# RWKV recurrence of a two-block model: token rows by chunk parity instead of by head, operands turned by whole 128x128 transposes, Gram products in two banks

## The reference, cut to what matters

```python
def frame_step(state, inp):                      # state: 64x64 for each head
    r_t, w_t, k_t, v_t, a_t, b_t = inp
    sa = einsum('bhvk,bhk->bhv', state, a_t)
    state = state * w_t + sa[..., None] * b_t + v_t[..., None] * k_t
    y_t = einsum('bhvk,bhk->bhv', state, r_t)
    return state, y_t
...
a, b = -kk, kk * ah                              # kk: k * k_k, normed in each head
y = (y - mean) * rsqrt(var + GN_EPS) * ln_w + ln_b
bonus = sum(rh * kh * r_k, axis=-1, keepdims=True) * vh
out = ((y + bonus) * g) @ w_o
```

## Time and profile before

| | us |
|---|---|
| median of 3 timed runs | 2976.05 (2974.72 to 2978.09) |
| span of the profiled execution | 2971.7 |
| TensorE matmul busy in it | 2867.8 (97%) |
| DVE, ACT, POOL busy | 1571.3, 1040.2, 185.7 |
| mean granted TensorE clock | 0.983 of full speed |
| one stage of the recurrence (stages 1 to 6) | 39.62 |
| TensorE busy in one such stage | 37.80 |
| DVE, ACT, POOL busy in it | 28.16, 12.02, 10.17 |

### The profile page before, as it was taken

How to read it: one execution, slowest core, us unless ns; L and a number is a source line. 1 busy time by engine, 2 the same in 40 slices (tenths; PEclk the granted TensorE clock), 3 DMA queues, 4 the chain that set the end, 5 groups by cost and what they waited for, 6 DMA issues and landing times.

```text
span 2971.7 us, 47531 instructions
## 1 busy us (share of the span) xinstructions
PE 2867.8 (97%) x21368; PEld 2323.2 (78%) x21368; DVE 1571.3 (53%) x2210; ACT 1040.2 (35%) x1333; POOL 185.7 (6%) x159
## 2 busy tenths in 40 slices
PE   7999999999899989999999999899999998999999
PEld 6878888778888877888777767678888786788887
DVE  7766554463677654323366666554344546454342
ACT  4225233343233235334343232242222446532221
POOL 0010000201322100000200000010000000100000
PEclk9999999999999999999999999899999999999999
DMA  7545544120000022222220111022322220222322
GB/s 280 217 170 197 199 178 173 66 99 29 17 3 3 18 102 84 99 99 99 82 72 30 51 36 44 15 100 82 110 95 83 100 86 1 85 100 70 122 82 68
DMA packets 41388, 270.70 MB, mean 91 GB/s; under 512 B 4576, under 2 KB 4832, under 8 KB 13280
## 3 DMA queue, kind: packets, MB, share of 16 engines
q1 hardware_dynamic: 40752, 266.11, 25.1%
q10 hardware_dynamic: 432, 1.54, 0.1%
HBM read 265.54 MB, written 2.10 MB: 90 GB/s over the span
## 4 chain that ended last, share of the span: by engine, by line
PE 89%; DVE 7%; ACT 3%; issue 1%; DMA 0%; SPq 0%; DVEq 0%; ACTq 0%
PE ps L696 21%; PE ps L702 21%; PE ps L697 21%; PE ps L2195 6%; PE ps L2973 1%; PE ps L1757 1%; PE ps L1740 1%; PE ps L1751 1%; PE ps L2301 1%; PE ps L2360 1%; PE ps L2354 1%; DVE WL L408 1%; PE ps L2329 1%; PE ps L2890 1%; PE ps L2877 1%
## 5 line engine op out<-in xcount | busy, mean ns | idle before, releaser
L696 PE MATMUL ps<-HH,WH 128*128 128x512 f32 x1928 | 765.9, 397 | 18.7 <-ACT HH L672 16.6
L697 PE MATMUL ps<-HH,WL 128*128 128x512 f32 x1928 | 756.7, 392 | 0.0
L702 PE MATMUL ps<-HL,WH 128*128 128x512 f32 x1928 | 730.1, 392 | 3.6 <-DVE HL L908 2.6
L408 DVE TENSOR_TENSOR WL<-ST,WH 128x2048 fp32r<-128x2048 f32 (+3 forms) x230 | 464.6, 2021 | 233.3 <-ACT WH L400 233.2
L400 ACT ACTIVATE WH<-ST 128x2048 fp32r<-128x2048 f32 (+1 forms) x211 | 383.4, 1817 | 302.8 <-PE ps L702 281.7
L696 PEld LDWEIGHTS ps<-HH,WH 128*128 128x128 f32 x1928 | 365.7, 190 | 102.2 <-issue 23.1
L702 PEld LDWEIGHTS ps<-HL,WH 128*128 128x128 f32 x1928 | 364.9, 189 | 84.4 <-DVE HL L908 4.1
L697 PEld LDWEIGHTS ps<-HH,WL 128*128 128x128 f32 x1928 | 365.8, 190 | 78.7 <-issue 3.8
L696 PE MATMUL ps<-GH,WH 128*128 128x512 f32 x928 | 361.0, 389 | 0.0
L697 PE MATMUL ps<-GH,WL 128*128 128x512 f32 x928 | 361.0, 389 | 0.0
L702 PE MATMUL ps<-GL,WH 128*128 128x512 f32 x928 | 359.7, 389 | 0.0
(11 more groups left out here) (390 smaller groups left out, 3485.7 us busy)
## 6 DMA issues: line engine op xcount, KB each, us to landing
ST<-w_m SPq DMA_DIRECT2D x64, 1024.0 KB, 4.9
ST<-w_gu SPq DMA_DIRECT2D x44, 1024.0 KB, 4.8
ST<-w_ada SPq DMA_DIRECT2D x40, 1024.0 KB, 6.1
ST<-w_dn SPq DMA_DIRECT2D x32, 704.0 KB, 4.0
ST<-w_gin SPq DMA_DIRECT2D x16, 1024.0 KB, 4.7
ST<-w_cin SPq DMA_DIRECT2D x12, 1024.0 KB, 5.0
ST<-w_rkv SPq DMA_DIRECT2D x12, 1024.0 KB, 4.7
W<-w_ada SPq DMA_DIRECT2D x16, 512.0 KB, 16.9
```

The source lines that it names most:

```text
L408: o = e.tensor_tensor(WL[:, j % 3, cut], ST[:, pos % 3, cut], WH[:, j % 3, cut].bitcast(F32), ALU.subtract)
L696: e.matmul(ps[:, :], wh[:, k, cs], H[:, k, :], start=(k == 0), stop=False)
L697: e.matmul(ps[:, :], wl[:, k, cs], H[:, k, :], start=False, stop=False)
L702: o = e.matmul(ps[:, :], wh[:, k, cs], L[:, k, :], start=False, stop=(k == kt - 1))
```

## The change

The change is all in the recurrence; the order of steps and the assignment of banks stay as they were.

1. After the operands are turned, a token's chunk parity, not its head, decides the partitions: even chunks on 0 to 63, odd chunks on 64 to 127. So four 128x128 transposes (two chunks and both heads each) take the place of 16 products with an identity, in `vt`, `at`, `bt`, `kt` and `yt`. `ss` becomes four products of 128x128 by 2 columns.
2. `gb`, `gk` and `mq` now cross from one layout into the other. Their two heads (or parities) write two banks, and each of the two groups writes half of both banks. The count that the readers wait for is raised for both banks in the last two chunks of the second group.
3. The start values of PN and PY are done in two rounds with a wait between them; the state steps do the PY products first; s7 has a wait before its last product.
4. The RI tile is laid out as three blocks of 8x64, and the DVE and POOL reads and writes of the Gram tiles go over every second chunk.

```diff
+        def across(g):
+            for c in range(8):
+                hh = (c + g) % 2
+                yield c, hh, c % 2, 2 * (c // 2) + hh
...
-            for c, hh in UNITS:
-                o = e.matmul(pre_b(m).tile(("ss", m))[rows(hh), c:c + 1], T0[rows(hh), 64 * c:64 * c + 64],
-                             tb("ones", rows(hh))[:, 0:1], start=True, stop=True)
+            for c2 in range(4):
+                o = e.matmul(pre_b(m).tile(("ss", m))[:, 2 * c2:2 * c2 + 2], T0[:, P * c2:P * c2 + P],
+                             tb("bones")[:, 0:P:64], start=True, stop=True)
...
             for g in range(2):
-                ps = prep_b.tile(("gb", m, g))
...
-                e.wait_ge(*prep_b.free(("gb", m, g)))
-                for c, hh in UNITS[8 * g:8 * g + 8]:
-                    o = e.matmul(ps[rows(hh), P * (c - 4 * g):P * (c - 4 * g) + P], BP[rows(hh), 64 * c:64 * c + 64],
-                                 RI[b][rows(hh), c, 64:192], start=True, stop=True)
-                o.then_inc(*scan_mm.up("gb", m, g))
+                for hh in range(2):
+                    e.wait_ge(*prep_b.free(("gb", m, hh)))
+                for c, hh, p, i in across(g):
+                    o = e.matmul(prep_b.tile(("gb", m, hh))[rows(p), P * (c // 2):P * (c // 2) + P],
+                                 BP[rows(hh), 64 * c:64 * c + 64], RI[b][rows(hh), 1:3, c, :], start=True, stop=True)
+                    if g and c > 5:
+                        o.then_inc(*scan_mm.up("gb", m, hh))
                 yield
...
-            for c, hh in UNITS:
-                o = e.matmul(prep_b.tile(("vt", m))[rows(hh), 64 * c:64 * c + 64], VV[rows(hh), m, 64 * c:64 * c + 64],
-                             tb("idk", rows(hh)), start=True, stop=True)
+            for c2 in range(4):
+                cs = slice(P * c2, P * c2 + P)
+                o = e.transpose(prep_b.tile(("vt", m))[:, cs], VV[:, m, cs], tb("ident"))
...
             e.wait_ge(*scan_vec.at("bt", m))
+            e.wait_ge(*scan_act.at("uw", m, 0))
+            e.wait_ge(*scan_vec.at("uw", m, 1))
             for g in range(2):
-                ps = prep_b.tile(("mq", m, g))
-                e.wait_ge(*prep_b.free(("mq", m, g)))
-                e.wait_ge(*(scan_vec.at("uw", m, 1) if g else scan_act.at("uw", m, 0)))
...
-            o.then_inc(*scan_mm.up("n", m))
-            yield
...
-            o.then_inc(*scan_mm.up("y0", m))
-            yield
+            for q in range(2):
+                if q:
+                    e.wait_ge(*scan_mm.at("n", m, 0))
+                for j in range(8):
+                    c, hh, i = 2 * (j // 2) + q, j % 2, j
+                    if c < 7:
+                        e.matmul(PN[rows(hh), 64 * c:64 * c + 64], BG[b][rows(q), i, 0:64], UW[rows(q), i, 0:64],
+                                 start=(c == 0), stop=False, skip_group_check=True)
+                    e.matmul(PY[rows(1 - q), 64 * i:64 * i + 64], BG[b][rows(1 - q), i, 64:128],
+                             UW[rows(1 - q), i, 0:64], start=(i == 0), stop=False, skip_group_check=True)
...
             for c in range(1, 8):
                 e.wait_ge(*scan_vec.at("s", m, c))
-                e.wait_ge(*scan_vec.at("mq", m, c // 4))
+                e.wait_ge(*scan_vec.at("mq", m, c % 2))
+                for d, hh in ((c, 0), (c - 1, 1)):
+                    if d > 0:
+                        i = 2 * (d // 2) + hh
+                        o = e.matmul(PY[rows(d % 2), 64 * i:64 * i + 64], MQ[rows(hh), d, 64:128], SA[rows(hh), d, :],
+                                     start=False, stop=True, skip_group_check=True)
...
+                else:
+                    o.then_inc(*scan_mm.up("y half", m))
+                    e.wait_ge(*scan_mm.at("y half", m))
+                    e.matmul(PY[rows(1), 64 * 7:64 * 7 + 64], MQ[rows(1), 7, 64:128], SA[rows(1), 7, :],
+                             start=False, stop=True, skip_group_check=True).then_inc(*scan_mm.up("y", m))
...
             for g in range(2):
                 e.wait_ge(*scan_mm.at("gb", m, g))
-                e.tensor_tensor(BG[b][:, 4 * g:4 * g + 4, 64:192], by4(prep_b.tile(("gb", m, g)), 4),
-                                INV[:, 4 * g:4 * g + 4, None].broadcast_to((P, 4, P)),
+                e.tensor_tensor(BG[b][:, g:8:2, 64:192], by4(prep_b.tile(("gb", m, g)), 4),
+                                INV[:, g:8:2, None].broadcast_to((P, 4, P)),
                                 ALU.mult).then_inc(*scan_vec.up("gb", m, g))
```

More of the change, by code:

```diff
@@ L1516, in tensor_pre @@
             for g in range(2):
-                ps = prep_b.tile(("gk", m, g))
                 e.wait_ge(*scan_pool.at("k", m))
[L1519 to L1523, removed]
+                for hh in range(2):
+                    e.wait_ge(*prep_b.free(("gk", m, hh)))
+                for c, hh, p, i in across(g):
+                    o = e.matmul(prep_b.tile(("gk", m, hh))[rows(p), P * (c // 2):P * (c // 2) + P],
+                                 KP[rows(hh), 64 * c:64 * c + 64], RI[b][rows(hh), 1:3, c, :], start=True, stop=True)
+                    if g and c > 5:
+                        o.then_inc(*scan_mm.up("gk", m, hh))
                 yield
             e.wait_ge(*prep_b.free(("at", m)))
-            for c, hh in UNITS:
-                o = e.matmul(prep_b.tile(("at", m))[rows(hh), 64 * c:64 * c + 64], RI[b][rows(hh), c, 128:192],
-                             tb("idk", rows(hh)), start=True, stop=True)
+            for c2 in range(4):
+                o = e.transpose(prep_b.tile(("at", m))[:, P * c2:P * c2 + P], RI[b][:, 2, 2 * c2:2 * c2 + 2, :].rearrange("p c t -> p (c t)"),
+                                tb("ident"))
             o.then_inc(*scan_mm.up("at", m))
             e.wait_ge(*prep_b.free(("bt", m)))
-            for c, hh in UNITS:
-                o = e.matmul(prep_b.tile(("bt", m))[rows(hh), 64 * c:64 * c + 64], BP[rows(hh), 64 * c:64 * c + 64],
-                             tb("idk", rows(hh)), start=True, stop=True)
+            for c2 in range(4):
+                cs = slice(P * c2, P * c2 + P)
+                o = e.transpose(prep_b.tile(("bt", m))[:, cs], BP[:, cs], tb("ident"))
             o.then_inc(*scan_mm.up("bt", m))
@@ L1544, in tensor_pre @@
             e.wait_ge(*prep_b.free(("kt", m)))
-            for c, hh in UNITS:
-                o = e.matmul(prep_b.tile(("kt", m))[rows(hh), 64 * c:64 * c + 64], KP[rows(hh), 64 * c:64 * c + 64],
-                             tb("idk", rows(hh)), start=True, stop=True)
+            for c2 in range(4):
+                cs = slice(P * c2, P * c2 + P)
+                o = e.transpose(prep_b.tile(("kt", m))[:, cs], KP[:, cs], tb("ident"))
             o.then_inc(*scan_mm.up("kt", m))
@@ L1799, in tensor_post @@
             e.wait_ge(*scan_vec.at("bt", m))
+            e.wait_ge(*scan_act.at("uw", m, 0))
+            e.wait_ge(*scan_vec.at("uw", m, 1))
             for g in range(2):
-                ps = prep_b.tile(("mq", m, g))
-                e.wait_ge(*prep_b.free(("mq", m, g)))
-                e.wait_ge(*(scan_vec.at("uw", m, 1) if g else scan_act.at("uw", m, 0)))
[L1804 to L1807, removed]
+                for p in range(2):
+                    e.wait_ge(*prep_b.free(("mq", m, p)))
+                for c, hh, p, i in across(g):
+                    o = e.matmul(prep_b.tile(("mq", m, p))[rows(hh), P * (c // 2):P * (c // 2) + P],
+                                 UW[rows(p), i, 64:128], BG[b][rows(p), i, 0:128], start=True, stop=True)
+                    if g and c > 5:
+                        o.then_inc(*scan_mm.up("mq", m, p))
                 yield
@@ L1818, in tensor_post @@
-            yield
-            if m:
-                e.wait_ge(*scan_vec.at("yn", m - 1))
-            for c, hh in UNITS:
-                e.matmul(PY[rows(hh), 64 * c:64 * c + 64], BG[b][rows(hh), c, 64:128], UW[rows(hh), c, 0:64],
-                         start=(c == 0), stop=False, skip_group_check=True)
-                o = e.matmul(PY[rows(hh), 64 * c:64 * c + 64], GK[b][rows(hh), c, 0:64], VT_[b][rows(hh), c, :],
-                             start=False, stop=(c == 0), skip_group_check=True)
@@ L1833, in tensor_post @@
+                for hh in range(2):
+                    if c < 7:
                         o = e.matmul(PN[rows(hh), 64 * c:64 * c + 64], MQ[rows(hh), c, 0:64], SA[rows(hh), c, :],
                                      start=False, stop=True, skip_group_check=True)
+                if c < 7:
                     o.then_inc(*scan_mm.up("s", m, c))
-                for hh in range(2):
-                    o = e.matmul(PY[rows(hh), 64 * c:64 * c + 64], MQ[rows(hh), c, 64:128], SA[rows(hh), c, :],
-                                 start=False, stop=True, skip_group_check=True)
@@ L1847, in tensor_post @@
             e.wait_ge(*scan_vec.at("yn", m))
-            for c, hh in UNITS:
```

(5 more changed lines are left out.)

44 lines of the change are left out of this document (23 added, 21 removed).

## The result

The changed kernel takes 2998.90 us (median of 5 runs, 2994.07 to 3001.89), the kernel before 2976.76 (5 runs, 2974.72 to 2978.09). The ratio is 1.0075, with a 95% interval of 1.0061 to 1.0090: slower by 22 us, where the prediction said 3007 and a range of 2993 to 3024. The profiled execution took 2996.21 us around a span of 2994.4, 22.7 more than the span before. So only 1.8 us lie outside the span; the rest of the 4.35 us by which the median of before stood above its profiled span is difference between executions, and it happened to be nearly the same here (2998.90 less 2994.4 is 4.5).

What follows compares the result with a forecast made beforehand. TensorE's instruction list plus waits was taken to bound a stage. Stages 1 to 6 at +3.91 each gave +23.5; with the other parts +27.9, plus +3 for the clock: span 3002.6, median 3007 us, range 2993 to 3024.

Steps and rivals of the forecast that it cites:

- VectorE's queue held by the late count: At gb and gk, TensorE stands while DVE does both groups' work in one piece: +4.29 us per stage.
- Stage 0: No state steps, so u itself waits at gb and gk, 1.56 us each; with transposes and ss, +2.3 us.
- stages 7 and 8: Stage 7 +0.7 us; stage 8 +2.1, from mq waiting for DVE's uw copy, PN/PY and longer state steps.
- Two of the signs that the prediction named: Signs of being right: stages of 43 to 44 us, and PN and PY taking 3.9 to 4.0.
- waits for itself: TensorE waits for its own products between PN and PY rounds and in s7: 0.24 us each, bounds 0.1 and 0.4.
- transposes: Four 128x128 transposes replace 16 identity products in vt, at, bt, kt and yt: -1.47 us per stage.
- new layout: `ss`, halves of PN/PY, third product of s7: Added TensorE work per stage: ss +0.25 us, half-empty PN/PY rounds +0.24, unpaired s7 product +0.12.
- The clock: The new wait at gb brings a fall of TensorE's clock in two stages, about 1.5 us each: +3 us.
- The waits do not appear: Rival: DVE catches up before TensorE needs SA(3), u4 and s7; 2974.5 us, not slower; 7%.
- The clock falls in most stages: Rival: falls at gb and at gk, ten more, +15 us, 3022; 15%.
- PN and PY of one column half take turns: Rival: PN and PY products in the same array columns alternate, 1.6 us per stage, +13, 3020; 8%.
- The two banks free the Gram products: Rival: parting two heads into two banks saves up to 2.6 us per stage, -21, 2986; 2%.

Runs made afterwards that it cites:

- experiment 1: Kernel before, with DVE waiting for the end of the second group of gb and of gk before taking out the first: 3007.98 us, ratio 1.0117.
- experiment 2: Kernel before, with the five groups of identity products replaced by four 128x128 transposes each (output not the reference's): 2960.13 us, ratio 0.9957.
- experiment 5: Kernel before, with TensorE waiting for itself between PN and PY products and ahead of the last PY product of s7: 2980.19 us, ratio 1.0021.
- experiment 7: Kernel before, with whole transposes, DVE waiting for both gb and gk groups, and TensorE's two waits for itself, without the new layout: 3005.16 us, ratio 1.0100.
- experiment 6: Kernel before, with TensorE doing both groups of gb, and of gk, in the first of their two steps: 2978.21 us, ratio 1.0008.
- experiment 4: Changed kernel, with TensorE doing both groups of gb, and of gk, in the first of their two steps: 2967.01 us, ratio to before 0.9967.

## Why the prediction was right, and where its sizes were not

**The mechanism is shown.** The prediction's deciding step, VectorE's queue held by the late count, gave +4.29 per stage; experiment 1 measures +4.29, and the starts along the chains of the earlier trace rows came out in the changed kernel within 0.01 us at four places. Stage 0 (two waits of 1.4 us), the first pair and stages 7 and 8 are each within 0.3. Of stage 8, `mq`'s wait is 3.04 instead of 2.03 us (+0.88 was forecast), and each of the six state steps waits 0.39 to 0.41 instead of 0.27 (+0.12 was forecast). Two of the signs that the prediction named for being right did not come: the stages measure 42.25 and not 43 to 44, and PN with PY 3.80 and not 3.9 to 4.0. That the time still lay in the range is partly luck: its lower end stood for a cheaper VectorE row and cheaper waits for itself, and neither came; the miss came from a term without bounds.

**The step that failed is the sum of TensorE's other work in stages 1 to 6.** It was put at +0.25 (`ss`) + 0.84 (PN, PY, s7) - 1.47 (transposes) = -0.38. Measured:

| per stage | forecast | measured | by |
|---|---|---|---|
| late counts | +4.29 | +4.29 | experiment 1 |
| transposes | -1.47 | -1.73 | experiment 2 |
| waits for itself | +0.48 | +0.70 | experiment 5 |
| new layout: `ss`, halves of PN/PY, third product of s7 | +0.61 | -0.62 | 42.25 - 42.87 |
| stage | +3.91 | +2.63 | 42.25 - 39.62 |

The last row but one is nearly the whole miss: 1.23 us per stage, 7.4 of the 8.0 us by which the recurrence came out below the forecast; the other two rows and the clock nearly cancel. The terms that the prediction named are not where it comes from: against experiment 7, `ss` with its entry costs 0.18 (forecast 0.25), and PN with PY and s7 are within 0.02 of it (forecast +0.36). The other 0.79 us are gained at `mq`, `gb`, `gk` and the state steps, for whose crossed products the prediction put nothing, as if a group began only when the one before had been issued. The trace shows otherwise. Timeline of the changed kernel at the end of `mq` (L1815), and at the end of PY (L1839):

```profile
887.33 0.76 PE L1815 MATMUL ps<-BG,UW 64*64 64x128 f32 x10
887.83 0.28 PE L1760 MATMUL ps<-UN,TT 64*64 64x64 f32 x2
887.92 0.28 PE L1815 MATMUL ps<-BG,UW 64*64 64x128 f32 x2
887.93 0.28 PE L1760 MATMUL ps<-UN,TT 64*64 64x64 f32 x4
...
893.54 0.22 PE L1839 MATMUL ps<-VTOK,GK 64*64 64x64 f32 x1
893.54 0.27 PE L1749 MATMUL ps<-TN,BG 64*64 64x64 f32 x1
893.60 0.22 PE L1839 MATMUL ps<-VTOK,GK 64*64 64x64 f32 x1
893.65 0.92 PE L1749 MATMUL ps<-TN,BG 64*64 64x64 f32 x26
```

The next group's products start while those of the group before still come. Start to start, against experiment 7: from the second `mq` group to `t` it is 0.40 less; from `u` to s1 0.10 less; the second `gb` group begins 0.23 sooner behind its state step and the second `gk` group 0.21 sooner behind `tt`; s3 and s5 take 0.17 and 0.18 instead of 0.28. Against it stand 0.10 for the first `gb` group and small ones of 0.01 to 0.07 around it and at s6. That it is the crossed layout which does this is argued from these rows and from experiment 6 against 4; the layout was not run alone.

PN with PY came out 0.18 us below its forecast (3.80, not 3.98). This is the break between its rounds:

```profile
889.74 0.22 PE L1830 MATMUL ps<-UW,BG 64*64 64x64 f32 x1
...
891.50 0.28 PE L1839 MATMUL ps<-VTOK,GK 64*64 64x64 f32 x2
891.73 0.27 PE L1830 MATMUL ps<-UW,BG 64*64 64x64 f32 x1
```

The first round issues for 1.87 us (889.74 to 891.61, 0.12 behind 891.50 with its two passes), 16 times 0.117, just as forecast; here the mixed corners overlap no further. So the half-empty rounds cost what was forecast. The second, up to `u` at 893.54, is 1.81 long. But the wait between them costs only 0.12 of its 0.24, where the same wait in experiment 5 cost 0.27, and 0.33 with what follows it. In the code it is for the last PN product, with one PY product still behind that; that this hides part of the wait is not shown by a run.

**The clock** fell in three of stages 1 to 6 (two forecast), each worth 0.90 us (1.5 forecast), 2.7 in all for 3. Of the changed kernel around one of them:

```profile
855.50:857.70 2.20, 0.00 (x1) 0.00 (x0) 2.12 (x5) 0.00 (x0) 1.26 (x1) 1.00 0.00 0
857.70:859.20 1.50, 1.49 (x42) 1.43 (x43) 0.91 (x3) 0.00 (x0) 0.87 (x1) 0.98 0.00 0
859.20:862.60 3.40, 3.40 (x45) 3.07 (x44) 2.10 (x4) 0.00 (x0) 0.39 (x1) 0.51 0.00 0
```

It follows the idle 2.2 us at s3, beginning 1.5 us behind it. In these stages s5's wait of 0.47 is gone, which is why they lose 0.90 and not the 1.45 of experiment 7, where the fall begins with s3 and s5 still waits 0.45. Experiment 1 has the steps between: a fall that begins 0.05 us behind s3 leaves s5's wait at 0.60 and costs 1.54 us, one at 0.75 leaves 0.24 and costs 1.19, one at 1.1 leaves nothing and costs 0.87. Why it falls after the same idle time in one stage and not in the next stays open; the prediction's "two stages" was a guess of the right size.

**The rivals.** *The waits do not appear*: they do. *The clock falls in most stages*: in three of six here; but in experiment 7, with the same stalls, in five, so the 15% were not too many. *PN and PY of one column half take turns*: no, 3.80 us with the wait. *The two banks free the Gram products*: a first `gb` group takes 0.98 instead of 0.88, so no. But experiments 4 and 6 show that there was something near it: both groups of `gb` at once, with `t` behind them, need 2.00 us instead of 2.68. Not the second bank but the crossed products do it, as far as these runs can tell, and the changed kernel's order leaves most of that unused, since `t`, `tt` and a state step stand between its two groups.

## What to carry to other kernels

When a change merges two completion counts into one, don't look at the producer: follow the consumer's queue from the first instruction that now waits, and add up what stands behind it until the engine that sets the pace is served. A sum made in that way was exact here. Price work on a saturated engine by a run or by a row of the same form and with the same neighbours: what the new layout did was put at +0.61 us per stage and came out at -0.62, most of it where one group runs into the next. And if a stall comes from where a wait stands in a queue, move the wait by one step before giving up the change: here that turned 22 us lost into 9 us gained.

## What the runs showed of the hardware

- Groups of 64x64 products, one within the corners 0 to 0 and 1 to 1 of the array and one across them, overlap further than two of the first kind when they stand in the queue together: from the first pass of `gb` to `tt` 2.00 us against 2.68, and 1.54 against 1.92 for the 32 passes of `gk` (experiments 4 and 6). The mixed products of PN and PY do not: 0.117 a pair in either layout. Records of the next group start before the last ones of the group before (887.83 against 888.14).
- A wait of TensorE for its own last product costs 0.39 - 0.12 = 0.27 us at the wait, and 0.35 per wait with what follows it, on a saturated engine (experiment 5); between the rounds of PN and PY in the changed kernel it costs 0.12.
- One and the same fall of the clock, 3.4 us at 0.51, costs 0.87 to 1.54 us, by how much of it is taken up by a wait behind it (experiment 1, stages 1 and 3).
- With stages of 38 us instead of 42 the recurrence of experiment 4 took 325.1 us instead of 358.3, 33.2 less, and the whole 31.9; but against experiment 2 (324.1) it is 1.0 longer in the recurrence and 6.9 in the median. The difference lies behind it, as far as one trace of each can tell: after 1100 us the trace of experiment 4 has 89.9 us at the lower clock, that of experiment 2 71.7 (the kernel before 78.5). Gains of a few us in one part can be lost in parts that nothing was changed in.
